# The last product of a two-block network with tokens on the partitions: weights in a ring of five places, one root for each token column

## The reference, cut to what matters

```python
def rms_norm_2(x, gain):
    xf = x.astype(jnp.float32)
    y = xf * lax.rsqrt(jnp.mean(xf * xf, axis=-1, keepdims=True) + EPS)
    return (y * gain.astype(jnp.float32)).astype(x.dtype)

def swiglu(x, w_gate, w_up, w_down):
    return (jax.nn.silu(x @ w_gate) * (x @ w_up)) @ w_down
...
        h = h + FFN_RESIDUAL_WEIGHT * rms_norm_2(swiglu(...), ffn2_post_norm[l])
```

## Time and profile before

| | us |
|---|---|
| median of three runs | 1937.56 (1936.98 to 1938.39) |
| the profiled execution, its time | 1936.09 |
| the profiled execution, its span | 1934.3 |
| TensorE busy | 1871.7 (97% of the span) |
| GpSimd busy | 1315.0 (68%) |
| VectorE busy | 826.8 (43%) |
| ScalarE busy | 473.7 (24%) |

### The profile page before, as it was taken

The page is one execution under the profiler, slowest core; times in us unless marked ns, Lnnn a source line. Parts: engine busy times, 40 slices in busy tenths (PEclk is TensorE's granted clock), DMA queues, the critical chain, the costliest instruction groups (busy, mean ns, idle before and its releaser), DMA issues.

```text
span 1934.3 us, 25617 instructions
## 1 busy us (share of the span) xinstructions
PE 1871.7 (97%) x8710; PEld 1520.1 (79%) x8710; DVE 826.8 (43%) x1335; ACT 473.7 (24%) x852; POOL 1315.0 (68%) x1281
## 2 busy tenths in 40 slices
PE   7999999999999999999999999899999999999996
PEld 6778888877778788888888777797876778888885
DVE  5156663168863422233057555633354262222002
ACT  3111111146641111111033244342423231111000
POOL 6666667757767777776677877362772677777664
PEclk9999999999999999999999999999999999999998
DMA  4222223232222322232233111000321212222321
GB/s 177 87 87 87 88 95 143 87 120 87 74 67 100 114 102 89 106 111 90 82 114 115 66 44 66 23 23 23 112 106 44 87 66 87 102 93 102 112 90 43
DMA packets 24545, 169.82 MB, mean 88 GB/s; under 512 B 2720, under 2 KB 2848, under 8 KB 6432
## 3 DMA queue, kind: packets, MB, share of 16 engines
q1 hardware_dynamic: 22896, 159.92, 23.0%
q10 hardware_dynamic: 1584, 9.05, 1.3%
HBM read 166.86 MB, written 2.10 MB: 87 GB/s over the span
## 4 chain that ended last, share of the span: by engine, by line
PE 92%; DVE 4%; ACT 2%; issue 1%; POOL 1%; DMA 0%; POOLq 0%; ACTq 0%; DVEq 0%
PE bank L383 22%; PE bank L385 22%; PE bank L384 22%; PE bank L421 2%; PE bank L422 2%; PE bank L423 2%; PE bank L1374 1%; PE bank L1376 1%; PE bank L1375 1%; PE bank L2025 1%; PE bank L1612 1%; PE bank L762 1%; PE bank L1586 1%; PE bank L2011 1%; PE bank L631 1%
## 5 line engine op out<-in xcount | busy, mean ns | idle before, releaser
L301 POOL TENSOR_TENSOR weights_lo<-raw_weights,weights_hi 128x512 fp32r<-128x512 f32 (+3 forms) x592 | 813.1, 1374 | 55.9 <-ACT weights_hi L318 7.5
L299 POOL TENSOR_SCALAR weights_hi<-raw_weights 128x512 fp32r<-128x512 f32 (+4 forms) x568 | 386.2, 680 | 452.1 <-PE bank L385 320.0
L383 PE MATMUL bank<-x_hi,weights_hi 128*128 128x512 f32 x1264 | 500.7, 396 | 0.2
L385 PE MATMUL bank<-x_lo,weights_hi 128*128 128x512 f32 x1264 | 492.1, 389 | 0.0
L384 PE MATMUL bank<-x_hi,weights_lo 128*128 128x512 f32 x1264 | 492.0, 389 | 0.0
L383 PEld LDWEIGHTS bank<-x_hi,weights_hi 128*128 128x128 f32 x1264 | 237.4, 188 | 53.3 <-issue 4.6
L384 PEld LDWEIGHTS bank<-x_hi,weights_lo 128*128 128x128 f32 x1264 | 237.4, 188 | 52.2 <-issue 3.8
L385 PEld LDWEIGHTS bank<-x_lo,weights_hi 128*128 128x128 f32 x1264 | 237.3, 188 | 49.5
L383 PE MATMUL bank<-ffn_y_hi,weights_hi 128*128 128x512 f32 x352 | 137.5, 391 | 1.6 <-DVE temps L1000 1.6
L384 PE MATMUL bank<-ffn_y_hi,weights_lo 128*128 128x512 f32 x352 | 137.0, 389 | 0.0
L385 PE MATMUL bank<-ffn_y_lo,weights_hi 128*128 128x512 f32 x352 | 137.0, 389 | 0.0
(11 more groups left out here) (420 smaller groups left out, 3035.0 us busy)
## 6 DMA issues: line engine op xcount, KB each, us to landing
raw_weights<-in_ffn_up SPq DMA_DIRECT2D x44, 1024.0 KB, 4.8
raw_weights<-in_ffn_down SPq DMA_DIRECT2D x16, 1408.0 KB, 5.9
raw_weights<-in_a_ug SPq DMA_DIRECT2D x16, 1024.0 KB, 4.7
raw_weights<-in_b_in SPq DMA_DIRECT2D x12, 1024.0 KB, 4.8
raw_weights<-in_a_out SPq DMA_DIRECT2D x8, 1024.0 KB, 4.7
raw_weights<-in_a_v SPq DMA_DIRECT2D x7, 1024.0 KB, 4.8
raw_weights<-in_b_out SPq DMA_DIRECT2D x8, 768.0 KB, 4.3
raw_weights<-in_gdn_qkv SPq DMA_DIRECT2D x6, 1024.0 KB, 4.8
```

Of the source, the lines that this page charges most:

```text
L299: nc.gpsimd.tensor_scalar(hi, raw, 1.0, 0.0, ALU.mult, ALU.add).then_inc(S("units_hi"), 1)
L301: nc.gpsimd.tensor_tensor(lo, raw, hi.bitcast(F32), ALU.subtract).then_inc(units_ready, 1)
L383: nc.tensor.matmul(ps, wh, xh[:, k, :], start=k == 0, stop=False)
L385: last = nc.tensor.matmul(ps, wh, xl[:, k, :], start=False, stop=k == last_k)
```

## The change

The last product is turned round. Its stationary operand is a block of 128 tokens of `Y_H` or `Y_L`, its moving operand 512 columns of weights, and its result has tokens on the partitions and 512 output features along the free axis. The 1024 output features are two halves, the 512 tokens four blocks, so there are eight results, one in each PSUM bank. The weights come in 44 units of 128x512 in 11 rounds of four units (22 units a half); they lie in a ring of five places in `WH` and `WL`. For the first 40 units TensorE takes all four token blocks for each unit; the last four units it takes token block by token block, so that the blocks of the second half end one after another. The number of matmuls and their sizes stay as they were: 44 x 4 x 3 = 528 of 128x512.

The sum of squares of a token is now an accumulator output of ScalarE's square of a bank, one column for each token block and half. ScalarE takes the square root of each column by itself, and VectorE makes the inverse and one Newton correction of it. The gain has to lie along the free axis, so ScalarE's queue loads it into all partitions ahead of `ffn2_up` (512 KB). The residual has to have tokens on its partitions: VectorE turns it round with 128 block transposes between `ffn2_up` and the first use. VectorE multiplies each bank by half the gain (`gain`), and for five of the eight pieces multiplies by the column and adds the residual (`finish`); for the three of `SCALED_BY_ACT`, ScalarE multiplies by the column and GpSimd adds the residual. The output tensor has another layout, and its stores keep their size (eight of 256 KB, pieces of 2 KB).

```diff
-    Phase("ffn2_up", 22, 16), Phase("ffn2_down", 8, 22),
+    Phase("ffn2_up", 22, 16), Phase("ffn2_down", 11, 16),
...
+        HALVES, WIDE, RING = 2, 512, 5
+        OT = place("out_tokens", 32, [TOK, HALVES, WIDE])
+        XT = place("residual_turned", 16, [KD, TOK, P])
+        GAINS = T[:, 4:6, :]
+        HALF0_SUMS, HALF1_SUMS, BASES, ROOTS, FINAL = SC[:, 64:68], SC[:, 68:72], SC[:, 72:76], SC[:, 76:80], SM[:, 0:4]
+        SCALED_BY_ACT = ((1, 0), (1, 1), (2, 1))
+        def final_bank(i, h):
+            return PS[4 * h + i]
+        def gained(i, h):
+            return OT[:, i, h, :] if (i, h) in SCALED_BY_ACT else final_bank(i, h)
+        def residual_turned(i, h):
+            return XT[:, 4 * h:4 * h + 4, i, :]
+        def half_done(i, h):
+            return PFD.used(5, 1) if h == 0 else PFD.used(PFD.rounds - 1, i)
+        def ring_slot(u):
+            return slice(4 * (u % RING), 4 * (u % RING) + 4)
+        def pool_final_weights(pool):
+            up = PH["ffn2_up"]
+            for u in range(4 * PFD.rounds):
+                r, j = divmod(u, 4)
+                if j == 0:
+                    loaded(pool, PFD, r % 2, r // 2)
+                if u < RING:
+                    pool.wait_ge(units_used, up.used(up.rounds - 1, (0, 1, 1, 2, 3)[u]))
+                else:
+                    pool.wait_ge(units_used, PFD.used((u - RING) // 4, (u - RING) % 4))
+                raw = RAW[:, r % 2, 4 * j:4 * j + 4, :]
+                hi, lo = WH[:, ring_slot(u), :], WL[:, ring_slot(u), :]
+                nc.gpsimd.tensor_scalar(hi, raw, 1.0, 0.0, ALU.mult, ALU.add).then_inc(S("units_hi"), 1)
+                pool.wait_ge(*due("units_hi", PFD.used(r, j)))
+                nc.gpsimd.tensor_tensor(lo, raw, hi.bitcast(F32), ALU.subtract).then_inc(units_ready, 1)
+        def pe_final_down(pe):
+            def products(u, i):
+                h, k = divmod(u, KF)
+                tok = tile_of(i)
+                wh = WH[:, ring_slot(u), :].rearrange("p t n -> p (t n)")
+                wl = WL[:, ring_slot(u), :].rearrange("p t n -> p (t n)")
+                bank = final_bank(i, h)
+                nc.tensor.matmul(bank, Y_H[:, k, tok], wh, start=k == 0, stop=False)
+                nc.tensor.matmul(bank, Y_H[:, k, tok], wl, start=False, stop=False)
+                return nc.tensor.matmul(bank, Y_L[:, k, tok], wh, start=False, stop=k == KF - 1)
+            last_round = 4 * (PFD.rounds - 1)
+            pe.wait_ge(*due("ffn2_tu", PH["ffn2_up"].rounds))
+            for u in range(last_round):
+                if u < KF:
+                    pe.wait_ge(*due("ffn2_yl", u + 1))
+                pe.wait_ge(units_ready, PFD.used(u // 4, u % 4))
+                for i in range(TOK):
+                    last = products(u, i)
+                last.then_inc(units_used, 1)
+            for i in range(TOK):
+                for u in range(last_round, HALVES * KF):
+                    if i == 0:
+                        pe.wait_ge(units_ready, PFD.used(u // 4, u % 4))
+                    last = products(u, i)
+                last.then_inc(units_used, 1)
+        def act_final_gains(act):
+            act.dma_start(GAINS.rearrange("p a n -> p (a n)"), dram["last_gain"].partition_broadcast(P)).then_inc(S("gains_in"), 16)
+        def act_final_down(act):
+            def square(i, h):
+                act.wait_ge(units_used, half_done(i, h))
+                sums = HALF1_SUMS if h else HALF0_SUMS
+                if h:
+                    act.wait_ge(*due("f2_sq", i + 1))
+                nc.scalar.activation(T[:, i, :], final_bank(i, h), ACT.Square, accum_out=sums[:, i:i + 1]).then_inc(S("f2_sq"), 1)
+            def root(i):
+                act.wait_ge(*due("f2_sq", TOK + i + 1))
+                nc.scalar.activation(ROOTS[:, i:i + 1], HALF1_SUMS[:, i:i + 1], ACT.Sqrt, bias=BASES[:, i:i + 1], scale=1.0 / D).then_inc(S("f2_rb"), 1)
+            def scale(i, h, nth_gained):
+                act.wait_ge(*due("f2_added", nth_gained))
+                act.wait_ge(*due("f2_diag", 3 + i))
+                nc.scalar.activation(OT[:, i, h, :], OT[:, i, h, :], ACT.Copy, scale=FINAL[:, i:i + 1]).then_inc(S("f2_rb"), 1)
+            for i in range(TOK):
+                square(i, 0)
+            act.wait_ge(*due("f2_diag", 2))
+            nc.scalar.activation(SC[:, 80:84], BASES, ACT.Sqrt)
+            square(0, 1)
+            root(0)
+            square(1, 1)
+            root(1)
+            scale(1, 0, 2)
+            square(2, 1)
+            root(2)
+            scale(1, 1, 6)
+            square(3, 1)
+            root(3)
+            scale(2, 1, 7)
+        def dve_final_down(dve, step):
+            for k in range(KD):
+                for fq in range(4):
+                    for tq in range(4):
+                        src = X[32 * fq:32 * fq + 32, k, :].rearrange("p (i t) -> p i t", t=P)[:, :, 32 * tq:32 * tq + 32]
+                        last = nc.vector.transpose(XT[32 * tq:32 * tq + 32, k, :, 32 * fq:32 * fq + 32], src)
+            last.then_inc(S("f2_diag"), 1)
+            NEGATED, Y = PS[1][:, 96:100], PS[1][:, 128:132]
+            W, Z = SC[:, 0:4], SC[:, 32:36]
+            def gain(i, h):
+                dve.wait_ge(units_used, half_done(i, h))
+                dve.wait_ge(*due("f2_sq", TOK * h + i + 1))
+                nc.vector.scalar_tensor_tensor(out=gained(i, h), in0=final_bank(i, h), scalar=0.5, in1=GAINS[:, h, :], op0=ALU.mult, op1=ALU.mult).then_inc(S("f2_added"), 1)
+            def column(i, nth_root):
+                c = slice(i, i + 1)
+                step(nc.vector.scalar_tensor_tensor(out=W[:, c], in0=HALF1_SUMS[:, c], scalar=-0.5 / D, in1=NEGATED[:, c], op0=ALU.mult, op1=ALU.add))
+                dve.wait_ge(*due("f2_rb", nth_root))
+                step(nc.vector.reciprocal(Y[:, c], ROOTS[:, c]))
+                step(nc.vector.tensor_tensor(Z[:, c], Y[:, c], W[:, c], ALU.mult))
+                step(nc.vector.tensor_tensor(Z[:, c], Z[:, c], Y[:, c], ALU.mult))
+                nc.vector.scalar_tensor_tensor(out=FINAL[:, c], in0=Z[:, c], scalar=1.5, in1=Y[:, c], op0=ALU.add, op1=ALU.mult).then_inc(S("f2_diag"), 1)
+            def finish(i, h, nth_gained):
+                dve.wait_ge(*due("f2_added", nth_gained))
+                dve.wait_ge(*due("f2_diag", 3 + i))
+                nc.vector.scalar_tensor_tensor(out=by_tile(OT[:, i, h, :]), in0=by_tile(gained(i, h)), scalar=FINAL[:, i:i + 1], in1=residual_turned(i, h), op0=ALU.mult, op1=ALU.add).then_inc(S("f2_x"), 1)
+            dve.wait_ge(*due("gains_in", 16))
+            for i in range(TOK):
+                gain(i, 0)
+            dve.wait_ge(*due("f2_sq", TOK))
+            nc.vector.tensor_scalar(BASES, HALF0_SUMS, 1.0 / D, RMS_EPS, ALU.mult, ALU.add).then_inc(S("f2_diag"), 1)
+            dve.wait_ge(*due("f2_diag", 2))
+            dve.wait_ge(*due("f2_added", 2))
+            step(nc.vector.tensor_scalar(NEGATED, BASES, -0.5, None, ALU.mult))
+            gain(0, 1)
+            column(0, 1)
+            finish(0, 0, 1)
+            finish(0, 1, 5)
+            gain(1, 1)
+            column(1, 2)
+            gain(2, 1)
+            column(2, 4)
+            finish(2, 0, 3)
+            gain(3, 1)
+            column(3, 6)
+            finish(3, 0, 4)
+            finish(3, 1, 8)
+        def pool_final_down(pool):
+            def add_residual(i, h, nth_scaled):
+                pool.wait_ge(*due("f2_rb", nth_scaled))
+                nc.gpsimd.tensor_tensor(by_tile(OT[:, i, h, :]), by_tile(OT[:, i, h, :]), residual_turned(i, h), ALU.add).then_inc(S("pool_x"), 1)
+            pool.wait_ge(*due("f2_diag", 1))
+            add_residual(1, 0, 3)
+            add_residual(1, 1, 5)
+            add_residual(2, 1, 7)
+        def sp_final_stores(sp):
+            pooled = len(POOL_TILES)
+            ready = {(0, 0): due("f2_x", 1), (0, 1): due("f2_x", 2), (1, 0): due("pool_x", pooled + 1), (2, 0): due("f2_x", 3), (1, 1): due("pool_x", pooled + 2),
+                     (3, 0): due("f2_x", 4), (2, 1): due("pool_x", pooled + 3), (3, 1): due("f2_x", 5)}
+            for i, h in ready:
+                sp.wait_ge(*ready[i, h])
+                sp.dma_start(out[:, i, h * WIDE:(h + 1) * WIDE], OT[:, i, h, :]).then_inc(S("stored"), 16)
+            sp.wait_ge(*due("stored", 16 * len(ready)))
...
...
-                pe_ffn_down(pe, "ffn2", "f2")
-                pe_sum_with_last(pe, "f2", ACC, T[:, 1, :], PS[7])
-                pe_spread(pe, "f2", DIAG, PS[6])
+                pe_final_down(pe)
...
+                act_final_gains(act)
                 act_ffn_up(act, "ffn2")
-                act_ffn_down(act, "ffn2", "f2")
-                act_rows(act, "f2", PS[6], RB[:, :])
+                act_final_down(act)
...
                 dve_ffn_up(dve, step, "ffn2")
-                dve_ffn_down(dve, step, "ffn2", "f2")
-                dve.wait_ge(*due("f2_rb", 1))
-                for k in range(KD):
```

(9 more changed lines are left out.)

26 lines of the change are left out of this document (16 added, 10 removed).

## The result

The changed kernel takes 1925.29 us (median of 4 runs, 1924.05 to 1927.36) beside 1937.97 for the kernel before (4 runs, 1936.98 to 1938.71): a ratio of 0.9937, 95% interval 0.9924 to 0.9950. In a second comparison it was 1925.83 (5 runs) beside 1936.96 (15 runs), 0.9942, 0.9928 to 0.9955. So it is 11 to 13 us faster. The forecast of 1927.5 had the sign and the place right; the first median lies 0.5 us under the range of 1925.8 to 1931.5, the second at its lower edge.

What follows compares the result with a forecast made beforehand. TensorE was taken as the bound nearly everywhere, so only the 18.46 us behind the last product could shrink. A tail of 8.39 us cut 10.1 from the median 1937.56, giving 1927.5 us, range 1925.8 to 1931.5.

Steps and rivals of the forecast that it cites:

- The product: Last product on TensorE: same 528 matmuls, 0.227 us each with no gap, its end kept at 1915.84; gain nothing.
- GpSimd's split: Splitting weight units on GpSimd beside the product: 1.99 us a unit against TensorE's 2.72; cost nothing if not disturbed.
- the ring: Five places for weight units: GpSimd gets up to four units ahead, the last ready 0.7 us before unit 40 begins.
- the load: The gain's 512 KB load beside `ffn2_up`, DMA engines busy 0.26 of the time, due 200 us later; cost nothing.
- The transposes: VectorE's 128 block transposes under the last product: 0.38 us each, 49 us in all (26 to 92), hidden.
- The tail: Time from the last product's end to the end of the span: 18.46 us before, predicted 8.39.
- E + 8.39: Predicted end of the span, E being the last product's end: last `finish` at E + 5.30, then 3.09 of store.
- the shortest tail I can defend: Lower limit behind the last product, with no queueing on VectorE: 7.2 us, which gives 1926.3 us.
- The sum: Whole kernel: span 1924.2 us against 1934.3, 10.1 less; off the median 1937.56 this gives 1927.5.
- Code and handovers: Rival: unrolled products, TensorE waits or a ScalarE table load in the tail eat part of the gain; 1931.5 us, chance 0.13.
- Transposes locking GpSimd out: Rival: beside the transposes GpSimd's split is blocked and TensorE starves; 24 us of missing units, 1951.5 us, chance 0.05.
- nothing coming of it: Rival: transposes held up by GpSimd, 0.90 us each, make VectorE late at block 0; 1935.5 us, chance 0.03.

Runs made afterwards that it cites:

- ring4: The changed kernel with a ring of four places instead of five; median 1926.18 us over 4 runs, ratio to before 0.9941, tail 7.07 us.
- transposes_x3: The changed kernel with each of VectorE's 128 block transposes done three times; 1939.59 us in 1 run, tail 22.18 us.
- before_const_wait: The kernel before, with ScalarE's last two rounds written outside the loop, so its wait is for a constant; 1936.38 us in 1 run, tail 17.93.
- dve_waits: The changed kernel with VectorE waiting for its own result behind each `gain` and `finish` of the second half; 1927.07 us in 1 run, tail 7.94.

## Why the prediction was right in its mechanism, and where its size was off

**The product, GpSimd's split, the ring, the load: right.** 119.61 us for 119.60, units of 0.63 and 1.30, no wait of TensorE. `ring4` shows that four places are one too few, by 0.4 us.

**The transposes: right, and cheaper than taken.** 0.303 us each, 0.316 from start to start and 40.5 in all, for 0.38 and 49; the row of 0.342 us alone would have given 44. The Trainium skill's (N + 151) / 0.96 (VectorE: DVE Perf Modes, The TRN2 errata), stated for a float32 addition of two inputs, gave an estimate of 0.29 and 37. That is 4% under the 0.303. GpSimd wasn't locked out: its units stayed at 0.63 and 1.30. `transposes_x3` shows by its 15.1 us that only the time they have hides them.

**The tail: the mechanism right, the size wrong. This is the step that failed.** The prediction gave "E + 8.39", and took as "the shortest tail I can defend" one with "no queueing at all on VectorE", 7.2. It is 7.07 with queueing. Its walk beside the trace, in us from E:

| | predicted | measured |
|---|---|---|
| block 0, `gain` starts | -7.05 | -7.30 |
| block 0, column ends | -5.32 | -5.77 |
| block 0, second `finish` ends | -3.74 | -4.24 |
| block 1, column ends | -2.01 | -2.81 |
| block 2, `gain` starts | -0.53 | -1.31 |
| last `finish` ends | +5.30 | +4.05 |
| span ends | +8.39 | +7.07 |

Two terms are too long, and each was measured by itself. "A `square` starts 0.29 us after its product" was read where the wait is for a register's value in a loop; for a constant outside one it is 0.04 (`before_const_wait`): 0.25 us. "`gain` takes 0.69 (as L1067) and 0.04 to the next", and `finish` likewise, holds where VectorE waits for its own result (`dve_waits`, last `finish` 1.03 us later); where the next instruction doesn't need it, it starts some 0.09 us before the recorded end of the last: from `gain` on, 0.61 us in place of 0.73, and from `finish` 0.67 in place of 0.79. Eight such places on the path make 1.0 us. With 0.07 less for the stores this is the 1.32. Smaller terms nearly cancel: a column takes 1.04 us up to the `finish` behind it, not 1.00, and `scale` 0.72, not 0.65, but block 2's square starts 0.09 us before the recorded end of that `scale`. Block 2's square, forecast "about 1.4 us later than its product allows", was 0.64 late (it starts at 1915.25, its product ends at 1914.61), by the same 0.8 us at block 1's column.

**The sum.** The tail took off 11.39 us, not the 10.1 of the sum; 1937.56 - 11.39 = 1926.2 would have been in the range. The other 0.9 us are runs: the four of the changed kernel spread over 3.3 us, their median was 1925.29 and that of five more 1925.83, and the medians of before were 1936.96 to 1937.97 in comparisons of 4 to 15 runs. That the predicted span, 1924.2, agrees with 1924.4 is partly luck: the product began 1.48 us later than in the profile of before, in code that is the same in both but for the gain's load. So the range was too tight at its lower end twice, in the tail and in what a few runs can show.

**The rivals.** Code and handovers: TensorE has no wait inside the product, and ScalarE's table load of 1.28 us runs at 1859.97, far ahead of the tail. Transposes locking GpSimd out, and nothing coming of it: both refuted by the rows on L1239 and L1166.

## What to carry to other kernels

When a norm or another whole-row result stands behind the last product, look at the order of the last units before the arithmetic: 6.8 to 8.2 of 11.4 us here come from ending the blocks one by one. Price a handover from a row of the same kind (a wait for a constant or a register, an instruction that needs the one before or doesn't), since nine handovers, eight of VectorE at some 0.12 us and one of ScalarE at 0.25, are the error of this forecast. Keep one operand of a small VectorE step in PSUM where GpSimd works beside it.

## What the runs showed of the hardware beyond that

The code ahead of the product, the same in all kernels but for the gain's load, took up to 1.9 us more or less from one profile to the next (the product's first start lay between 1795.65 and 1797.58 in 14 profiles, in the two of the kernel before at 1795.85 and 1796.68). A part of it is TensorE's clock. Windows of before, then of after:

```profile
1250.00:1255.00 5.00, 2.12 (x16) 1.57 (x15) 5.00 (x6) 0.00 (x0) 3.61 (x3) 1.00 0.00 0
1255.00:1260.00 5.00, 3.47 (x29) 3.12 (x29) 2.51 (x3) 1.79 (x3) 3.62 (x4) 1.00 0.00 0
```
```profile
1250.00:1255.00 5.00, 2.14 (x17) 1.52 (x15) 4.45 (x6) 0.00 (x0) 3.62 (x4) 0.88 0.00 0
1255.00:1260.00 5.00, 5.00 (x22) 4.82 (x23) 3.23 (x3) 1.20 (x2) 3.62 (x4) 0.50 0.00 0
```

In both, TensorE was busy for 2.1 of the 5 us before 1255. Then it was granted 2.4 GHz in the one, and 1.2 GHz for 5 us in the other, with 22 matmuls instead of 29. The windows aren't quite the same work: after its last gap TensorE starts again at 1254.29 in the one (L2011) and at 1254.99 in the other (L2198, the same products), where the clock had fallen by then. From this start to that of the products behind them (L2025, L2212) are 5.68 and 6.49 us, so the lower level cost 0.8 us here. Why the same work meets either level isn't settled. ScalarE's root of one column takes 0.29 us (L1210), longer than the four-column root of 0.20 us (L1220). The first adds a column from memory (`BASES`) and the second does not, but no run parts the two.
